# Shifting the matmul operands of a two-block transformer kernel against each other in on-chip memory

## The reference

```python
h_lat = _modulate(xl, mod_l[0], mod_l[1])            # normed stream, 512 x 1024
a, g, q, k, v, o, gates = _split_cols(h @ w_in, AB_SIZES)
...
y = jnp.concatenate([u, hm], axis=-1) @ w_out        # second operand of a layer
xl = xl + mod_l[2] * y_lat
g, val = jnp.split(h @ w_in, 2, axis=-1)             # feed-forward, width 2816
return (jax.nn.gelu(_dwconv(g, conv_w, conv_b), approximate=True) * val) @ w_out
```

## Time and profile before

| | us |
|---|---|
| median of 3 runs | 3673.59 |
| lowest and highest | 3673.03, 3673.9 |
| profiled execution, whole | 3674.51 |
| its span, first to last instruction | 3672.7 |
| PE busy | 3572.8 (97%) |
| DVE busy | 1983.1 (54%) |
| ACT busy | 1620.1 (44%) |
| POOL busy | 1325.2 (36%) |

### The profile page before, as it was taken

One profiled execution on the slowest core, in us unless ns is written; L12 is line 12 of the kernel. 1 busy time (PEld: TensorE's weight loads), 2 busy tenths in 40 slices (PEclk: granted clock), 3 DMA queues, 4 the chain that ended last, 5 costly groups with the idle time before them and its releaser, 6 DMA issues.

```text
span 3672.7 us, 56483 instructions
## 1 busy us (share of the span) xinstructions
PE 3572.8 (97%) x21302; PEld 2938.1 (80%) x21302; DVE 1983.1 (54%) x3008; ACT 1620.1 (44%) x2819; POOL 1325.2 (36%) x614
## 2 busy tenths in 40 slices
PE   7999999999999999999999999999999999999998
PEld 5875788888877777888777778789977777878997
DVE  4857553333357775343555653557555665356555
ACT  4344432221266663332655552445455555335444
POOL 2530333232331113444422334355543233344555
PEclk9999999999999999999999999999999999999999
DMA  5368221111220002322312222232322222222332
GB/s 211 115 230 309 92 75 63 63 63 63 69 81 24 24 24 91 99 97 92 102 59 70 70 70 94 77 105 87 115 87 69 70 70 70 86 93 75 110 104 92
DMA packets 85382, 335.84 MB, mean 91 GB/s; under 512 B 9648, under 2 KB 9776, under 8 KB 78640
## 3 DMA queue, kind: packets, MB, share of 16 engines
q1 hardware_dynamic: 84448, 330.79, 26.7%
q10 hardware_dynamic: 720, 2.10, 0.2%
HBM read 329.18 MB, written 2.10 MB: 90 GB/s over the span
## 4 chain that ended last, share of the span: by engine, by line
issue 44%; PE 36%; POOL 14%; DVE 3%; ACT 1%; POOLq 0%; DMA 0%; ACTq 0%; DVEq 0%; SPq 0%
POOL w_lo L3550 14%; PE pB L287 7%; PE pB L288 7%; PE pB L289 6%; PE pT L1095 2%; PE pT L1096 1%; PE pT L1097 1%; PE pT L289 1%; PE pT L288 1%; PE pT L287 1%; PE pO L287 1%; PE pO L289 1%; PE pO L288 1%; PE pO L1097 1%; PE pO L1095 1%
## 5 line engine op out<-in xcount | busy, mean ns | idle before, releaser
L3550 POOL TENSOR_TENSOR w_lo<-w_raw,w_hi 128x1024 fp32r<-128x1024 f32 x452 | 1106.9, 2452 | 2071.2 <-ACT w_hi L333 2070.1
L333 ACT ACTIVATE w_hi<-w_raw 128x1024 fp32r<-128x1024 f32 x452 | 476.5, 1055 | 561.0 <-PE pB L289 365.0
L287 PE MATMUL pB<-h_hi,w_hi 128*128 128x512 f32 x1540 | 607.7, 395 | 18.7 <-DVE h_lo L477 6.0
L288 PE MATMUL pB<-h_lo,w_hi 128*128 128x512 f32 x1540 | 600.3, 390 | 0.0
L289 PE MATMUL pB<-h_hi,w_lo 128*128 128x512 f32 x1540 | 599.5, 389 | 0.0
L287 PE MATMUL pB<-b_hi,w_hi 128*128 128x512 f32 (+1 forms) x1084 | 399.2, 368 | 3.6 <-DVE b_lo L1307 1.6
L288 PE MATMUL pB<-b_lo,w_hi 128*128 128x512 f32 (+1 forms) x1084 | 394.9, 364 | 0.0
L289 PE MATMUL pB<-b_hi,w_lo 128*128 128x512 f32 (+1 forms) x1084 | 394.6, 364 | 0.0
L287 PEld LDWEIGHTS pB<-h_hi,w_hi 128*128 128x128 f32 x1540 | 290.0, 188 | 94.4 <-issue 15.5
L289 PEld LDWEIGHTS pB<-h_hi,w_lo 128*128 128x128 f32 x1540 | 289.8, 188 | 61.0
L288 PEld LDWEIGHTS pB<-h_lo,w_hi 128*128 128x128 f32 x1540 | 290.1, 188 | 58.0 <-issue 1.2
(11 more groups left out here) (673 smaller groups left out, 7085.1 us busy)
## 6 DMA issues: line engine op xcount, KB each, us to landing
w_raw<-stream SPq DMA_DIRECT2D x520, 512.0 KB, 3.3
under<-ada SPq DMA_DIRECT2D x42, 1024.0 KB, 5.6
arena<-ada SPq DMA_DIRECT2D x6, 1024.0 KB, 17.4
x<-xT SPq DMA_DIRECT2D x1, 2048.0 KB, 9.2
out<-x SPq DMA_DIRECT2D x8, 256.0 KB, 2.1
xc<-cT SPq DMA_DIRECT2D x1, 1024.0 KB, 26.5
arena<-bmask ACTq DMA_DIRECT2D x1, 1024.0 KB, 4.9
w_hi<-arena SPq DMA_DIRECT2D x4, 192.0 KB, 8.4
```

Of the source, the lines that this page charges most:

```text
L287: pe.matmul(dst, lh, rh, start=(begin and k == 0), stop=False)
L288: pe.matmul(dst, lh, rl, start=False, stop=False)
L333: act.activation(w_hi[:, s, :], w_raw[:, s, :], ACT.Copy).then_inc(hi_ready, 1)
L3550: pool.tensor_tensor(w_lo[:, s, :], w_raw[:, s, :], w_hi[:, s, :].bitcast(F32), ALU.subtract).then_inc(lo_ready, 1)
```

## The change

Nine empty tensors are put between others. No instruction is added, removed or moved, on any engine; the rows of all five engines read the same before and after, and only addresses differ.

- 320 bytes ahead of `h_hi`; 64 bytes each between `h_hi`, `h_lo`, `b_hi`, `b_lo`; 512 bytes between `b_lo` and `w_raw`.
- 64 bytes ahead of the arena; 64 bytes each between `xh_hi`, `xh_lo`, `xb_hi`, `xb_lo`.

The empty tensors ahead of the weights sum to 1,024 bytes, so the weights keep their place modulo 1,024, and so do `attA`, `attP`, `attT`, `hsum`, `xc_t` and `combo_rest`. The new distances to the weights, modulo 1,024, are: `h_hi` 320, `h_lo` 384, `b_hi` 448, `b_lo` 512; `xh_hi` (and all of the arena) 64, `xh_lo` 128, `xb_hi` 192, `xb_lo` 256. `under` gets 16 more columns in each of its four rows, so that each still begins where its buffer of `h` or `b` begins.

```diff
+        sb("place_h", [P, 80])
+        with nc.sbuf_tensor("under", [P, 4, KD * T + 16], F32) as under:
             pass
-        h_hi, h_lo = sb("h_hi", [P, KD * T], F32R), sb("h_lo", [P, KD * T], F32R)
-        b_hi, b_lo = sb("b_hi", [P, KD * T], F32R), sb("b_lo", [P, KD * T], F32R)
+        h_hi, _ = sb("h_hi", [P, KD * T], F32R), sb("place_h_lo", [P, 16])
+        h_lo, _ = sb("h_lo", [P, KD * T], F32R), sb("place_b_hi", [P, 16])
+        b_hi, _ = sb("b_hi", [P, KD * T], F32R), sb("place_b_lo", [P, 16])
+        b_lo, _ = sb("b_lo", [P, KD * T], F32R), sb("place_w", [P, 128])
         w_raw = sb("w_raw", [P, SLOTS + 1, KD * P])
...
+        sb("place_arena", [P, 16])
         with nc.sbuf_tensor("arena", [P, ARENA], F32) as arena:
             pass
...
-        xh_hi, xh_lo = sb("xh_hi", [P, KD * C], F32R), sb("xh_lo", [P, KD * C], F32R)
-        xb_hi, xb_lo = sb("xb_hi", [P, KD * C], F32R), sb("xb_lo", [P, KD * C], F32R)
-        sb("arena_rest", [P, ARENA - 4 * KD * C])
+        xh_hi, _ = sb("xh_hi", [P, KD * C], F32R), sb("place_xh_lo", [P, 16])
+        xh_lo, _ = sb("xh_lo", [P, KD * C], F32R), sb("place_xb_hi", [P, 16])
+        xb_hi, _ = sb("xb_hi", [P, KD * C], F32R), sb("place_xb_lo", [P, 16])
+        xb_lo = sb("xb_lo", [P, KD * C], F32R)
+        sb("arena_rest", [P, ARENA - 4 * KD * C - 48])
...
-        spare = [under[:, 1, 0:half], under[:, 2, half:], under[:, 3, half:]]
+        spare = [under[:, 1, 0:half], under[:, 2, half:KD * T], under[:, 3, half:KD * T]]
```

More of the change, by code:

```diff
@@ L150, in program @@
         xc = sb("xc", [P, KD, C])
-        with nc.sbuf_tensor("under", [P, 4, KD * T], F32) as under:
-            pass
-        h_hi, h_lo = sb("h_hi", [P, KD * T], F32R), sb("h_lo", [P, KD * T], F32R)
-        b_hi, b_lo = sb("b_hi", [P, KD * T], F32R), sb("b_lo", [P, KD * T], F32R)
+        sb("place_h", [P, 80])
+        with nc.sbuf_tensor("under", [P, 4, KD * T + 16], F32) as under:
+            pass
+        h_hi, _ = sb("h_hi", [P, KD * T], F32R), sb("place_h_lo", [P, 16])
+        h_lo, _ = sb("h_lo", [P, KD * T], F32R), sb("place_b_hi", [P, 16])
+        b_hi, _ = sb("b_hi", [P, KD * T], F32R), sb("place_b_lo", [P, 16])
+        b_lo, _ = sb("b_lo", [P, KD * T], F32R), sb("place_w", [P, 128])
         w_raw = sb("w_raw", [P, SLOTS + 1, KD * P])
```

## The result

| | before | after |
|---|---|---|
| median of 3 runs, us | 3673.59 | 3711.99 |
| lowest and highest, us | 3673.03, 3673.9 | 3704.05, 3712.07 |
| profiled execution: whole, span, us | 3674.51, 3672.7 | 3704.05, 3702.2 |

The change made the kernel slower: the ratio of after to before is 1.0098, with a 95% interval from 1.0075 to 1.0121. That lies above the predicted 3625 us and also above the range's upper end of 3705. The three runs of after spread over 8 us, and the profiled one is the fastest of them: its span is 3702.2 us at a mean granted clock of 0.997, and the two others have 3710.3 and 3710.2 us at 0.995, the clock of the trace of before.

The account below looks back on a forecast made before the run. PE was taken as the bound: 12,180 matmuls x 4.2 ns = 51.2 us, 95% of it on the path, 48.6 us, off 3674.5 gives 3625.9; forecast 3625 us, 8-in-10 range 3556 to 3705.

Parts of the forecast that it names:

- What bounds the kernel: PE, busy 3572.8 of 3672.7 us; shortening the time between matmul starts shortens the span nearly one for one.
- the operand's place matters: Fast product, 256 columns: 120.0 ns at distance 0, 113.3 at 192, so 6.7 ns hang on the address.
- The rival of no change: Every placement costs the same or the new distances equal 0, so 3667 to 3681 us; chance 0.14.
- The price per matmul: All 12,180 matmuls with a new distance gain 4.2 ns each, the middle of -1.7 and -6.7: 51.2 us.
- The loss bound of +5.3: Upper bound of loss per matmul, from the first five of a chunk at 232 ns against 226.7.
- Distance 0 as the worst place: Argument for most of the surplus going (3552 to 3596 us, chance 0.20): both readers start at the same place.
- The pattern cannot distinguish 512 bytes: Weight blocks lie 512 bytes apart, yet starts keep one distance over even and odd blocks alike.
- `b_lo` at 512 "is no change": Second operand: the 1176 of 3528 matmuls that stream `b_lo` were counted at nothing, leaving 2352.
- Line 2848: Part of the normed stream: 3 x 800 = 2400 matmuls, priced at the same 4.2 ns gain as the others.
- The rival "slower": Products with unequal high and low distances may never settle: +5.3 ns each, 3735 us, half of it 3704; chance 0.23.
- 216 ns: Distance between plain float32 matmul starts at 256 columns, taken as the floor for float32r at 512 columns.
- The forecast's 10.5 ns a matmul: Surplus of a 512-column float32r matmul (226.7 ns) over the float32 floor (216), the upper bound of the gain.

Follow-up runs that it names:

- scan: Kernel of TensorE alone, 79 sections of 48 float32r matmuls, each at other operand distances; 512 columns took 226.7 ns at distance 0, 233.3 at 192.
- equal_a: Against the change: high and low parts at one distance, `h` 192, `b` 320, `xh` 64, `xb` 128; 3702.76 us, ratio 1.0077 to the kernel before.
- whole256: Against the change: `h_hi` and `b_hi` at 256, `h_lo` and `b_lo` at 512, context as in the change; 3668.9 us, ratio 0.9991 to before.
- scan2: TensorE alone, 97 sections of 48 matmuls with PE resting between them, distances in 8-byte steps; at 512 columns only 0 and 112 reached 226.7 ns.

## Why the prediction was wrong

**What bounds the kernel: right.** PE alone sets the time; the earlier trace rows read that way, and the +31.4 us of PE busy became +29.5 us of span. Of the 31.4 us, 94% reached the span, where I had taken 95%; since the two traces differ in clock, that close agreement is partly luck. No other engine's cost showed.

**That the operand's place matters: right.** That nanoseconds hang on the address held in every run. The rival of no change falls: with all other engines idle the same matmul takes 226.7 or 233.3 ns, by the distance alone. The Trainium skill ("SBUF — State Buffer", the section "Who interferes with whom") gives TensorE two independent read ports, one for the moving operand and one for the weights. That every placement costs the same was my conclusion from it; the measurement differs, and the measurement decides.

**The price per matmul: wrong, and this is the step that failed.** I took -1.7 and -6.7 ns from the earlier trace rows, which are matmuls of 256 columns, and gave the middle, -4.2, to 12,180 matmuls of which 8860 stream 512 columns (7020 on `h`, 1840 on `b`). No row of before had 512 columns at any distance but 0. At 256 columns the sign carried: context 120.0 to 117.8, -2.2 ns, and `h` in the fast product the same. At 512 the price was +4.9 ns for `h` and +7.7 for `b` in the settled part of a chunk. Over whole chunks, 17.9 us on 4656 and 18.2 on 2784 are +3.8 and +6.5 ns: the first matmuls of a chunk were already dearer before. The loss bound of +5.3 was near this; the mistake was to give an unmeasured width the sign of the measured one.

**Distance 0 as the worst place: wrong.** That "distance 0 has the readers start at the same place, which looks like the worst choice" was an argument without a row. No place tried is better at 512 columns in either scan, and of the multiples of 64 it is the worst at 256 columns.

**"The pattern cannot distinguish 512 bytes": right**, the period is in fact 256. **That `b_lo` at 512 "is no change": wrong** all the same. The first sentence holds for a matmul among its like; `b_lo` stands between two matmuls on `b_hi` at 448, and the settled step of the three is 234.4 each. The mean duration of its matmuls (line 294) rose by more than that of line 295's on `b_hi`: from 364 to 371 ns, against 364 to 366. The 1176 matmuls that I counted at nothing belonged in the sum.

**Line 2848: counted and nearly without effect.** I priced its 2400 matmuls like the others. Their steps sum to 574.8 us before and 576.3 after: 240 ns each, dearer than the settled step in either layout. They run with other matmuls between them. The median step rose from 229 to 232 ns, and longer ones fell (the 90th percentile from 240 to 238); that they have no settled step to lose would fit, but no run tests it.

**The rival "slower": near in size, wrong in cause.** It gave +5.3 ns and 3735 us, and half of it 3704, beside 3712 measured. Its place and its threshold (a mean over 227.3 ns) were right. Its mechanism was that unequal parts never settle; they do settle (at 231.9), equal parts are slow too (equal_a), and parts apart by 256 bytes are fast (whole256). Only that inequality has a price of its own came out, in the pairs of scan. It had 0.23, and I let the range end at 3705, at half its price; the ends of the price should have been kept.

```profile
680.17 20.88 PE L62 MATMUL pD<-f_mm,f_ww 128*128 128x256 f32 x96
700.89 20.88 PE L62 MATMUL pA<-f_mm,f_ww 128*128 128x256 f32 x96
```

20.72 us from one section to the next over 96 records are 215.8 ns a record. So 216 ns, which the prediction found to agree with the columns' rule, is the pace of half a matmul of another format, and no evidence for what a float32r matmul can reach: no distance tried, equal or not, went below 226.7 at 512 columns. The forecast's 10.5 ns a matmul were won by no placement here.

## What to carry to other kernels

A price read at one width is not evidence for another, not even in its sign: before summing a per-matmul change over thousands, look whether any row has the same width, and if none has, keep both signs in the range. For products of three float32r matmuls with 512 streamed columns, keep every streamed operand at a multiple of 256 bytes from the weights, and the high and low weights so from each other; 256-column streams win 2 ns at 64. When a busy engine is the bound and no wait moved, subtract starts in the timeline: that showed where this loss lies. Before a few us of two traces are compared, compare the time that each ran at half clock.

## What the runs showed of the hardware

- The step of float32r matmuls depends on where the streamed operand lies relative to the weights, modulo 256 bytes: 226.7 to 240.0 ns at 512 columns, 113.3 to 120.0 at 256 (192 bytes gave 117.8 in scan and 113.3 in scan2); at 128 columns it stood at 111.7 at each distance tried (0, 64, 128, 192).
- The surplus over the columns' own time is no constant: 13.3 ns at 384 and 512 columns, up to 19.2 between them (229.2 at 504, over 210.0).
- The step that a run of matmuls settles into can depend on what ran ahead of it (512 columns at 112 bytes: 226.7 or 231.1; at 64 bytes: 228.9 or 233.3), and shorter weight loads do not remove the surplus (228.9 to 233.3 at distance 0 with 16 to 112 columns, against 226.7 with 128).
- No variant beat the kernel before by more than the measurement can tell. The nearest, whole256, has 0.9991 [0.9982, 1.0001]; its trace has -2.8 us in the context, which the cause explains. Most of the other -7 us is the clock: its trace ran 13.6 us less at 1.2 GHz, and at full clock `h`, `b`, fast product and rest together differ by -1.6 us.
- The granted clock sets much of the spread of one kernel: of the 21 runs of before beside whole256, the one with 0.998 and a time of 3668.33 us and the one with 0.993 and 3684.64 lie 16 us apart.
